# A two-block transformer on one core: the residual kept with tokens on partitions, output projections turned to match

## The reference, cut to what matters

```
h   = rmsnorm(x, pre_mix_g)
proj = h @ w_in              # q, k, v of three attentions, and three gates
mix = ga * (ya @ w_oa) + gb * (yb @ w_ob) + gc * (yc @ w_oc)
x   = x + rmsnorm(mix @ w_out, post_mix_g)
h   = rmsnorm(x, pre_ffn_g)
x   = x + rmsnorm(conv_ffn(h, w_up, conv_w, conv_b, w_down), post_ffn_g)
```

```
h = concatenate([meta, x])
for i in range(2):
    y = rmsnorm(h, pre_norm[i])
    y = attention_mixer(y, ...) if i == 0 else gla_mixer(y, ...)
    h = h + rmsnorm(y, post_norm[i])
return h[16:]
```

## Time and profile before

| | |
|---|---|
| median of three runs | 2507.98 us |
| the profiled execution | 2503.05 us |
| its span, first to last instruction | 2501.3 us |
| TensorE, VectorE, ScalarE, GpSimd busy | 96%, 57%, 48%, 14% |
| mean granted TensorE clock | 0.985 |
| mean HBM traffic | 159 GB/s |

### The profile page before, as it was taken

One profiled execution on the slowest core, in us unless ns is written; L12 is line 12 of the kernel. 1 busy time (PEld: TensorE's weight loads), 2 busy tenths in 40 slices (PEclk: granted clock), 3 DMA queues, 4 the chain that ended last, 5 costly groups with the idle time before them and its releaser, 6 DMA issues.

```text
span 2501.3 us, 48097 instructions
## 1 busy us (share of the span) xinstructions
PE 2412.9 (96%) x18529; PEld 2292.7 (92%) x18529; DVE 1437.6 (57%) x1757; ACT 1189.8 (48%) x1762; POOL 356.2 (14%) x306
## 2 busy tenths in 40 slices
PE   8999999999979999999999979999999899999998
PEld 7898999999969999999999969998889889998876
DVE  5555644467476666666544457885554463555544
ACT  5444544454444444444444434444445443564443
POOL 0000000024132221222100013220002220001210
PEclk9999999999989999999999989999999999999999
DMA  8444466646535556555555544443334455453333
GB/s 287 144 138 132 143 185 185 184 148 200 185 100 186 185 178 190 185 185 178 192 184 185 183 132 136 151 151 119 100 100 164 151 167 164 137 151 110 109 137 143
DMA packets 253947, 399.07 MB, mean 160 GB/s; under 512 B 15071, under 2 KB 111324, under 8 KB 253180
## 3 DMA queue, kind: packets, MB, share of 16 engines
q1 hardware_dynamic: 252452, 393.53, 49.7%
q10 hardware_dynamic: 1384, 3.99, 0.4%
HBM read 393.24 MB, written 4.22 MB: 159 GB/s over the span
## 4 chain that ended last, share of the span: by engine, by line
PE 90%; DVE 5%; ACT 3%; issue 2%; POOL 1%; DMA 0%; ACTq 0%; DVEq 0%; POOLq 0%; SPq 0%
PE bank L1550 74%; PE bank L2049 3%; PE bank L1565 2%; DVE wlo L1043 1%; PE bank L2015 1%; PE bank L1853 1%; PE bank L1822 1%; ACT whi L548 1%; DVE xT L1157 1%; DVE tmp L1146 1%; PE bank L1976 1%; PE bank L1924 0%; PE bank L1797 0%; PE bank L1791 0%; DVE rstd L1131 0%
## 5 line engine op out<-in xcount | busy, mean ns | idle before, releaser
L1043 DVE TENSOR_TENSOR wlo<-raw,whi 128x1024 fp32r<-128x1024 f32 x749 | 957.4, 1288 | 865.9 <-ACT whi L548 864.3
L1550 PE MATMUL bank<-ahi,whi 128*128 128x256 f32 (+1 forms) x4480 | 1291.9, 288 | 16.5 <-POOL alo L2060 12.7
L1550 PE MATMUL bank<-ahi,wlo 128*128 128x256 f32 (+1 forms) x4480 | 1275.3, 285 | 0.0
L1550 PE MATMUL bank<-alo,whi 128*128 128x256 f32 (+1 forms) x4480 | 1272.6, 284 | 0.0
L548 ACT ACTIVATE whi<-raw 128x1024 fp32r<-128x1024 f32 x749 | 787.6, 1057 | 792.3 <-PE bank L1550 733.3
L1550 PEld LDWEIGHTS bank<-ahi,whi 128*128 128x128 f32 x4480 | 850.1, 190 | 36.4 <-issue 29.7
L1550 PEld LDWEIGHTS bank<-ahi,wlo 128*128 128x128 f32 x4480 | 849.1, 190 | 0.0
L1550 PEld LDWEIGHTS bank<-alo,whi 128*128 128x128 f32 x4480 | 846.7, 189 | 1.4 <-issue 0.2
L1550 PE MATMUL bank<-ghi,whi 128*128 128x256 f32 x704 | 198.1, 281 | 1.1 <-ACT yT_ffn L786 1.1
L1550 PE MATMUL bank<-glo,whi 128*128 128x256 f32 x704 | 197.8, 281 | 0.0
L1550 PE MATMUL bank<-ghi,wlo 128*128 128x256 f32 x704 | 197.8, 281 | 0.0
(11 more groups left out here) (300 smaller groups left out, 2251.0 us busy)
## 6 DMA issues: line engine op xcount, KB each, us to landing
raw<-in_w_up SPq DMA_DIRECT2D x176, 512.0 KB, 4.6
raw<-in_w_in SPq DMA_DIRECT2D x156, 512.0 KB, 3.6
raw<-in_attn_w_in SPq DMA_DIRECT2D x96, 512.0 KB, 3.8
raw<-in_gla_w_in SPq DMA_DIRECT2D x96, 512.0 KB, 3.8
raw<-in_w_down SPq DMA_DIRECT2D x80, 512.0 KB, 4.3
raw<-in_w_out SPq DMA_DIRECT2D x32, 512.0 KB, 4.4
raw<-in_attn_w_out SPq DMA_DIRECT2D x32, 512.0 KB, 3.7
raw<-in_gla_w_out SPq DMA_DIRECT2D x32, 512.0 KB, 3.7
```

What stands on the lines that cost most here:

```text
L1043: dve.tensor_tensor(wlo[:, u % RING, :], raw[:, u % RAW, :], whi[:, u % RING, :].bitcast(F32), ALU.subtract).then_inc(wlo_ready, 1)
L1550: mm = pe.matmul(bank[:, base + t, 0:T], w[wp][:, k, col:col + P], rhs(ap, k0 + k), start=begins and k == 0 and (wp, ap) == (0, 0), stop=e ...
```

## The change

The residual stays as it comes, with tokens on partitions (`xtok`). The decays' buffer `cum` and `xtok` share a place. The meta tokens' residual is apart, features on partitions (`xm`).

- `wout` and `down` are computed by the new `rows_of_unit`: tokens stationary, 512 weight columns moving, two pairs of PSUM banks in turn. `down` becomes 2 trips of 48 units, `wout` 2 of 16, the same weights in the same amount. The trips are written out.
- Each chunk of rows is squared by ScalarE with a sum along the row and multiplied by the gain, which is loaded as a row for all partitions (`load_gain`), by VectorE.
- `aout` keeps features on partitions, with a plain copy out; TensorE turns each chunk's 256 tokens into rows (`turn_chunk`), the first three beside later units.
- The norms between the stages (`norm(b)` on each engine) work on rows with one number per partition. The normalised rows are turned in eight groups of four transposes, four of them ahead of the next stage and four beside its first units. ScalarE and VectorE make the high and low parts from PSUM. GpSimd has no part.
- The meta tokens' norm before the second block is made beside `wout`; their residual update and next norm beside the second trip of `gqk`.
- The first two trips of `gqk` (q) run on 256 tokens; x is parked as it lies, and the turns of x at the start and before parking go.
- `lr` takes both ranks as 32 stationary columns at once, 48 matmuls; `up_w` gets 32 rows, of which GpSimd clears the half that the other direction would use.
- The rope tables' loads move into `aqk`, the masks' and rank weights' loads behind the first trip of `gqk`.

```diff
-          ("wout", 4, 8, 1), ("up", 11, 16, 2), ("down", 4, 24, 1), ("aqk", 6, 8, 1), ("av", 2, 8, 1),
+          ("wout", 2, 16, 2), ("up", 11, 16, 2), ("down", 2, 48, 2), ("aqk", 6, 8, 1), ("av", 2, 8, 1),
...
+        XN_PIECES = ((0, 0, D), (1, 0, 512), (1, 512, 1024), (1, 1024, D))
+        N_XN = [3 + 4 * (b - 1) for b in range(4)]
...
+        def row_bank(b, c, tt):
+
+            return 2 * (c % 2) + tt + (4 if b == 3 else 0)
```

On ScalarE:

```diff
+            def rows_squared(b, c, tt):
+
+                act.activation(y_rows(b, tt, 512 * c, 512), bank[:, row_bank(b, c, tt), :].rearrange("p (k f) -> p k f", f=P),
+                               ACT.Square, accum_out=ynsum[:, tt, c:c + 1]).then_inc(y_squared, 1)
...
+            def norm(b):
+
+                y_mean(b, 0)
+                x_square(b, 0, 0)
+                y_mean(b, 1)
+                x_square(b, 0, 1)
+                x_square(b, 1, 0)
+                x_mean(b, 0)
+                x_square(b, 1, 1)
+                x_mean(b, 1)
+                for g in range(4):
+                    norm_hi(b, g)
...
+            def load_gain(b, src, offset, dst):
+
+                act.dma_start(dst, bass.AP(tensor=src.tensor, offset=offset, ap=[[0, P], [P, KD], [1, P]])).then_inc(row_gain, 16)
...
+            load_gain(1, A["post_mix_g"], 0, gain_rows(1, 0, D))
             load_roots(1)
-            stream("wout", y_out(1))
-            norm_after(1)
-            norm_before(1)
...
+            for i in range(TRIPS["wout"]):
+                trip("wout", i, rows_out_of(1), after=beside_wout)
+            norm(1)
...
+            load_gain(3, A["post_norm_2"], 0, gain_rows(3, 0, D))
             load_roots(3)
...
+            for i in range(TRIPS["aout"]):
+                trip("aout", i, feature_out(yT, T2, ACT.Copy), after=lambda i, j: turned_squares(i - 1) if i and j == 2 else None)
+            turned_squares(3)
+            norm(3)
```

On VectorE:

```diff
+            def rows_gained(b, c, tt):
+
+                if c == 0 and tt == 0:
+                    dve.wait_ge(row_gain, 16 * b)
+                dve.wait_ge(y_squared, 8 * (b - 1) + 2 * c + tt + 1)
+                y = dve.tensor_tensor(y_rows(b, tt, 512 * c, 512), bank[:, row_bank(b, c, tt), :].rearrange("p (k f) -> p k f", f=P),
+                                      gain_rows(b, 512 * c, 512), ALU.mult)
...
+                dve.scalar_tensor_tensor(x_rows(tt, c0, n), y_rows(b, tt, c0, n), xstat[:, 0, tt:tt + 1], x_rows(tt, c0, n),
+                                         ALU.mult, ALU.add).then_inc(x_updated, 1)
...
+            def norm_lo(b, g):
+
+                dve.wait_ge(hhi_ready, KD * b + 2 * g + 2)
+                for k in (2 * g, 2 * g + 1):
+                    dve.scalar_tensor_tensor(ha(alo, k, 0, TB), turned(k), par[:, G_PRE[b] + k:G_PRE[b] + k + 1],
+                                             ha(ahi, k, 0, TB).bitcast(F32), ALU.mult, ALU.subtract).then_inc(act_ready, 1)
+
+            def norm(b):
+
+                rows_gained(b, 3, 0)
+                y_summed(b, 0)
+                y_inverse(b, 0)
+                x_update(b, 0, 0)
+                rows_gained(b, 3, 1)
+                y_summed(b, 1)
+                x_update(b, 0, 1)
+                y_inverse(b, 1)
+                x_update(b, 1, 0)
+                x_summed(b, 0)
+                x_update(b, 1, 1)
+                x_normed(b, 0)
+                x_summed(b, 1)
+                x_normed(b, 1)
+                x_normed(b, 2)
+                for g in range(4):
+                    if g == 2:
+                        x_normed(b, 3)
+                    norm_lo(b, g)
```

On TensorE:

```diff
+                        for wp, ap in PASSES:
+                            tokens_of = ha(src[ap], k0 + k, tt * P, P) if b == 1 else src[ap][:, k0 + k, tt * P:(tt + 1) * P]
+                            mm = pe.matmul(bank[:, row_bank(b, c, tt), :], tokens_of, w[wp][:, k, :],
+                                           start=begins and k == 0 and (wp, ap) == (0, 0),
+                                           stop=ends and k == nk - 1 and wp == 1)
+                    mm.then_inc(tile_pass, 2)
...
+            def norm_turn(b, g):
+
+                pe.wait_ge(xn_ready, N_XN[b] + (2 if g < 2 else 3 if g < 4 else 4))
+                if g >= 4:
+                    pe.wait_ge(act_ready, LO[f"norm{b}"] + 2 * (g - 4) + 2)
+                turn_rows(xnorm[b], g).then_inc(xn_turned, 1)
...
+            def turn_y(c, t):
+
+                pe.wait_ge(acc_free, 4 * (C0["aout"] + c) + t + 1)
+                for tt in range(2):
+                    mm = pe.transpose(bank[:, row_bank(3, c, tt), t * P:(t + 1) * P], yT[:, 4 * c + t, tt * P:(tt + 1) * P], ident[:, :])
+                    if t == 3:
+                        mm.then_inc(y_turned, 1)
...
+            for i in range(TRIPS["aout"]):
+                for j in range(UNITS["aout"]):
+                    features("aout", i, j, z2_part, T2, LO["z2"] if i == 0 else None)
+                    if i and j == 1:
+                        turn_chunk(i - 1)
+            turn_chunk(3)
+            norm(3)
...
             for j in range(UNITS["gqk"]):
-                features("gqk", 0, j, model(T2), T2, LO["norm3"])
...
+                features("gqk", 0, j, model(TB), TB, LO["norm3"])
+                if j < 4:
+                    norm_turn(3, 4 + j)
+            for j in range(UNITS["gqk"]):
+                features("gqk", 1, j, model(TB), TB)
+                beside_gqk(j)
+            pe.wait_ge(m_ready, 2)
+            with pe.Fori(2, TRIPS["gqk"]) as i:
                 for j in range(UNITS["gqk"]):
-                    features("gqk", i, j, model(T2), T2, LO["norm3"])
+                    features("gqk", i, j, model(T2), T2)
...
+            bank_free("lr", c, 0, 0)
+            for k in range(KD):
+                cols = slice(2 * k * GL_RANK, 2 * (k + 1) * GL_RANK)
+                for wp, ap in PASSES:
+                    mm = pe.matmul(bank[0:2 * GL_RANK, 0, 0:T2], (whi, wlo)[wp][:, u % RING, cols], ha((ahi, alo)[ap], k, 0, T2),
+                                   start=k == 0 and (wp, ap) == (0, 0), stop=k == KD - 1 and wp == 1)
+            mm.then_inc(tile_pass, 4)
```

More of the change, by code:

```diff
@@ new lines, in later_lo, with rows_out_of, read_out, meta_sum @@
+            def later_lo(b):
+                return lambda i, j: norm_lo(b, 4 + j) if j < 4 else None
+            def rows_out_of(b):
+                def read_out(i, chunk, u, n):
+                    if 2 * i + chunk < 3:
+                        for tt in range(2):
+                            rows_gained(b, 2 * i + chunk, tt)
+                return read_out
+            def meta_sum(n):
+                dve.wait_ge(m_squared, n + 1)
+                dve.tensor_reduce(mstat[:, 0, :], sqm[:, :, :].rearrange("p k t -> p t k"), AX.X, ALU.add).then_inc(m_sum, 1)
@@ L1252, in _, with beside_wout @@
             stream("oabc", mix_out)
-            stream("wout")
-            norm_after(1)
-            norm_before(1)
+            def beside_wout(i, j):
+                if (i, j) == (0, 9):
+                    meta_sum(0)
+                if (i, j) == (0, 12):
+                    meta_norm(0, 2)
+                if (i, j) == (0, 13):
+                    meta_lo(1)
+            for i in range(TRIPS["wout"]):
+                trip("wout", i, rows_out_of(1), after=beside_wout)
+            norm(1)
             def up_out(i, chunk, u, n):
@@ L1271, in up_out @@
                     dve.tensor_tensor(pr[:, t, :], cv[:, t, :], cv[:, 2 + t, :], ALU.mult).then_inc(ff_prod, 1)
-            stream("up", up_out, split_before=1)
-            stream("down")
-            norm_after(2)
-            norm_before(2)
+            trip("up", 0, up_out, after=later_lo(1))
+            with dve.Fori(1, TRIPS["up"]) as i:
+                trip("up", i, up_out)
+            stream("down", rows_out_of(2))
+            norm(2)
             def qk_norm(i, j):
@@ L1339, in attend @@
                     gated((s - 17) // 2)
-            trip("aqk", 0, split_before=1)
+            trip("aqk", 0, after=later_lo(2))
             trip("aqk", 1, after=qk_norm)
@@ L1350, in _, with beside_aout, beside_gqk @@
                 gated(h)
-            stream("aout")
-            norm_after(3)
-            norm_before(3)
-            stream("gqk", split_before=1)
+            def beside_aout(i, j):
+                if i and j == 3:
+                    for tt in range(2):
+                        rows_gained(3, i - 1, tt)
+            for i in range(TRIPS["aout"]):
+                trip("aout", i, after=beside_aout)
+            norm(3)
+            def beside_gqk(i, j):
+                if j == 0:
+                    meta_sum(1)
+                if j == 2:
+                    meta_inverse(1)
+                    y = yT[:, :, TB:T2]
+                    dve.tensor_tensor(y, y, over_meta(mstat[:, 1, :]), ALU.mult).then_inc(m_scaled, 1)
+                    dve.wait_ge(m_scaled, 2)
```

(33 more changed lines are left out.)

492 lines of the change are left out of this document (241 added, 251 removed).

## The result

The changed kernel took 2450.38 us, median of four runs (2448.90 to 2451.00), the kernel before 2508.61 beside it (four runs, 2506.97 to 2509.62): a ratio of 0.977, 95% interval 0.9758 to 0.9782. The forecast was 2450.5. It is right in the total and in most of what makes it up, but it hit so closely because two errors cancel: the profiled execution became 2503.05 - 2450.43 = 52.6 us shorter, not 57.6, and the 4.9 us that I put between profiled execution and median are not there in the changed kernel (2450.43 against 2450.38).

A forecast was written before the change was run, and what follows sets the result against it. TensorE, 96% busy, was taken as the bound, other engines counting only where it waits, chiefly at three residual norms. Savings of 57.6 us took 2503.05 to 2445.4; with 4.9 to the median, forecast 2450.5, range 2440 to 2467.

The forecast's parts named there:

- stop after w_out: TensorE's wait at the residual norm behind w_out, with its added turns and slow clock: 15.6 us against 28.4, 12.8 saved.
- stop after w_down: The residual norm's wait behind w_down: same steps and widths as after w_out, 15.6 us against 29.2, 13.6 saved.
- stop after attention, turns: Wait behind the attention output: 17.1 us against 31.1, less 2.6 for turning three chunks beside later units, 11.4 saved.
- lost: Work added on a late path: gain-load issues at the starts of w_out and attention output, a late ones-matmul; 1.3 us lost.
- E: Modelled end of the last matmul before each stop: its start plus 0.28 or 0.29 us.
- the tail's projection is that form: 0.2327 each: w_out and w_down with 512 moving columns would run at the tail's pace, saving 1.9 and 6.8 us.
- one ones-matmul can come 0.4 late: In the meta tokens' own norm, beside units, VectorE has a subtraction ahead of the sum; 0.4 us lost.
- the median is 4.9 above it: Runs' median 2507.98 against profiled execution 2503.05 before the change; the same 4.9 us was added to 2445.4, giving 2450.4.
- Half-closed gaps: Rival: hand-overs and serial VectorE updates make each of the three gaps 6 us longer, 2468.5 us; chance 0.11.
- a third stop that stays: Rival: after the attention output, last-chunk turning and ScalarE's late feeding of gqk lose the 11.4 us, 2462; chance 0.07.
- The clock's rival: Rival: nothing behind the gaps runs at the 1.2 GHz level, transposes quicker too; some 2 us each, 2445; chance 0.04.
- The weight stream: Rival: wide units wait for weights, their copy and subtraction; at 3.5 us per unit 2535.5, slower; chance 0.02.

The follow-up runs named there:

- e1_narrow: The changed kernel with each 512-column matmul in w_out and w_down issued as two of 256; 2451.57 us, ratio 0.9781 to the kernel before.
- e5_places: The changed kernel with a weight copy and subtraction and the meta tokens' ones-matmuls moved later, and gate ranks in their own bank; 2444.68 us, ratio 0.9760.
- e7_before_parts: The kernel before with only the one-pass gate ranks and the last q without meta tokens; 2496.63 us, ratio 0.9971.
- e6_issues: The changed kernel with the first row of gains loaded by four DMA issues of ScalarE instead of one, same bytes; 2454.48 us, one sample.
- e2_pool: The changed kernel, in effect unchanged, since the function with the intended GpSimd adds was never called; 2450.74 us, ratio 0.9777.
- e11_after_again: The changed kernel without edits, run again beside the kernel before on one chip; 2448.84 us, ratio 0.9787.

## Why the prediction was right, and where it wasn't

Term by term, forecast and trace of the changed kernel (us saved):

```
stop after w_out                 12.8    12.9
stop after w_down                13.6    13.2
stop after attention, turns      11.4    11.7
w_out wide                        1.9     1.8
w_down wide                       6.8     5.4
last q                            2.9     2.4
gate ranks                        6.0     5.3
turns of x at the start           3.5     3.5
lost                             -1.3    -3.1
sum                              57.6    53.1
```

The span became 52.7 shorter.

*What bounds the kernel, and the stops.* Shown. Seven tenths of the gain are there, each within 0.4 of its term, since the kernel's own tail and start had every piece of the new chain. Of what went, GpSimd's share is shown by itself: 7.5 us in the stops by taking it away in the old layout, 8 by bringing it back in the new. That the rest is the rest of the old chain (one inversion for all tokens, the ones-matmuls, the squares behind the updates) is read from the traces; no run takes it away by itself.

*The second stop, 0.4 short.* Its terms were taken over from the first. But w_down ends in units of half size, so the next stage's weight copy and its subtraction (1.23 on VectorE) fall between the last matmuls and the first gained tile: the first update starts at E + 2.3 for E + 1.1. Moving them gave 0.8 back.

*The wide form in w_down, 1.4 short, and for the wrong reason.* The step "the tail's projection is that form: 0.2327 each" held for w_out (0.2321). w_down's wide matmuls stand 0.2333 apart, 246.4 for the 245.7 of the sum; the other 0.7 is that all of w_down had taken 251.8 and not four times a quarter with its break, 252.5, since the last quarter has none. And e1_narrow shows that width gives it nothing. The Trainium skill, "TensorE: Matmul & The Clock Gate", part 1, has 2.5 ns for each matmul; w_out shows 5.2 for a pair and w_down 0, so neither the page's figure nor my 5 describes both.

*The meta tokens' ones-matmuls, 2.7 short.* The failed step is "one ones-matmul can come 0.4 late". There are two, and TensorE's breaks around them are 1.3 and 1.9 us long: the six loads and the parking keep ScalarE from 1995.65 to 1999.2, its weight copy and the square follow, VectorE puts a subtraction ahead of the sum, and the second norm hangs on the first through ScalarE and VectorE. I had used the covering of those issues by the split units and not followed what stood behind them.

*The gate ranks, 0.7 short.* The 48 matmuls take the 6.0 forecast. Going from two banks to one, the next stage's first tile waits for ScalarE's copy, which I had not costed; an own bank takes it away (e5_places).

*The last q, 0.5 short.* e7_before_parts gives 2.6 for the 2.9 in the kernel before. Where the rest went was not followed.

*The gains' issues, 0.9 too pessimistic.* "0.45 is lost" twice: nothing was; at w_out's start the issue begins beside the activation ahead of it (e6_issues).

*From span to median.* The step "the median is 4.9 above it" carried a difference of one kernel's single profiled execution to the other. It gave back what the terms above had too much. The medians of before over the study, 2502.7 to 2508.6, show how little such a difference is a property of the kernel. Measured again beside the kernel before, the same change gave 54.6 us (e2_pool) and 53.9 (e11_after_again), nearer to the trace's 53 than to the 58 that I forecast and first measured; the close hit of the total is luck.

*The rivals.* Half-closed gaps and a third stop that stays: refuted by the trace. The clock's rival was mis-placed: the changed kernel does come out of each stop at 1.2 GHz, but that level governs the sixteen turns more than the matmuls behind them, and holding the clock is worth 4.3 us over the three stops by the trace. How many of the first matmuls still run at it differs between samples of one kernel (e2_pool), 1 us in a stop. The weight stream never became the bound: w_down runs at 0.2333 with no subtraction waited for.

## What to carry to other kernels

When a chain crosses engines in a stop of TensorE, look for the same pieces elsewhere in the same kernel and cost it from their rows: the three stops came within 0.4 us each. Small work that is put beside units must be followed to its last consumer, with everything queued ahead of it on each engine, a DMA issue and a weight subtraction included; it was there that the forecast lost most. And check which edits could be had without the change: one engine's share moved gave 10 us in the kernel before, and three small edits gave 10 more in the changed one.

## What the runs showed of the hardware

- Two SBUF operands on VectorE beside a GpSimd add of other buffers: 3.02 and 2.25 us for 1.28, each ending 1.1 us behind the end of a GpSimd instruction; with one operand from PSUM 0.68, unchanged.
- A DMA issue of ScalarE starts with the activation ahead of it: one of 0.38 us behind an activation of 0.42 is free, four take 2.0 and hold the queue 1.6.
- A pause of TensorE of 3.7 us was followed by a stretch at a granted clock of 0.65, 1.5 us dearer, in one execution; pauses of 2.1 at the same place, in eight profiles, were not. Sixteen turns take 3.2 us at 1.2 GHz and 1.7 at 2.4.
- Matmuls with the tokens stationary: 116.7 ns for 256 columns in w_down, 118.5 in w_out, and 233.3 and 232.1 for 512. The difference is open.
